# A transformer trunk on one core: residual and transposes between stages in steps of four tiles, norm-weight products in SBUF, turned tiles in PSUM banks 4 to 7

## The reference

```python
def rms_norm(x, g, eps=RMS_EPS):
    xf = x.astype(jnp.float32)
    y = xf * lax.rsqrt(jnp.mean(xf * xf, axis=-1, keepdims=True) + eps)
    return (y * g.astype(jnp.float32)).astype(x.dtype)
...
def conv_ffn(x, w_in, w_dw, w_out):
    u = causal_dwconv(x @ w_in, w_dw)
    g, up = jnp.split(u, 2, axis=-1)
    return (jax.nn.silu(g) * up) @ w_out

def per_layer_embed(h, p_i, pre_g, w_gate, b_gate, w_proj, post_g):
    gate = jax.nn.sigmoid(rms_norm(h, pre_g) @ w_gate + b_gate)
    return rms_norm(gate * (p_i @ w_proj), post_g)
...
    h = x
    for i in range(DEPTH):
        hn = rms_norm(h, pre_mix_g[i])
...
        h = h + rms_norm(y, post_mix_g[i])
        f = conv_ffn(rms_norm(h, pre_ffn_g[i]), ffn_w_in[i], ffn_w_dw[i], ffn_w_out[i])
        h = h + rms_norm(f, post_ffn_g[i])
        h = h + per_layer_embed(h, p[i], ple_pre_g[i], ple_w_gate[i], ple_b_gate[i],
                                ple_w_proj[i], ple_post_g[i])
    return h
```

## Time and profile before

| | us |
|---|---|
| median of 3 runs (2521.71 to 2524.05) | 2522.75 |
| span of the profiled execution, first to last instruction | 2521.0 |
| TensorE busy with products | 2450.2 |
| VectorE busy | 1666.8 |
| ScalarE busy | 1307.0 |

### The profile page before, as it was taken

The page is one execution under the profiler, slowest core; times in us unless marked ns, Lnnn a source line. Parts: engine busy times, 40 slices in busy tenths (PEclk is TensorE's granted clock), DMA queues, the critical chain, the costliest instruction groups (busy, mean ns, idle before and its releaser), DMA issues.

```text
span 2521.0 us, 40724 instructions
## 1 busy us (share of the span) xinstructions
PE 2450.2 (97%) x12610; PEld 2087.9 (83%) x12610; DVE 1666.8 (66%) x2183; ACT 1307.0 (52%) x1882; POOL 27.6 (1%) x49
## 2 busy tenths in 40 slices
PE   7999899999999999999999999999999999999997
PEld 6888787888888888887788887888888888788876
DVE  6889766777777754446665577567777777544465
ACT  6555545555555543436454455465656666433363
POOL 1000000000000000000000000000000000000000
PEclk9999999999999999999999999999999999999999
DMA  6444264666655665555555543646666666655554
GB/s 214 134 128 136 71 195 147 195 191 188 187 185 185 199 201 186 192 189 193 179 180 183 186 151 131 203 150 189 197 191 187 189 185 185 211 189 187 188 195 139
DMA packets 365325, 448.28 MB, mean 178 GB/s; under 512 B 27084, under 2 KB 273726, under 8 KB 364076
## 3 DMA queue, kind: packets, MB, share of 16 engines
q1 hardware_dynamic: 363452, 436.75, 54.5%
q0 software_dynamic: 1776, 10.41, 1.3%
HBM read 444.95 MB, written 2.10 MB: 177 GB/s over the span
## 4 chain that ended last, share of the span: by engine, by line
PE 88%; issue 5%; DVE 3%; ACT 2%; DMA 1%; DVEq 0%; SPq 0%; POOL 0%; ACTq 0%; POOLq 0%
PE ps L1274 34%; PE ps L1276 17%; PE ps L1309 11%; PE ps L1311 11%; PE ps L1310 11%; PE ps L1347 2%; PE ps L1254 1%; DVE v_conv L936 1%; DVE w_lo L809 1%; PE ps L1413 0%; PE ps L1427 0%; DVE h L861 0%; ACT w_hi L504 0%; DMA gain<-in_post_ffn_g 0%; ACT v_conv L610 0%
## 5 line engine op out<-in xcount | busy, mean ns | idle before, releaser
L809 DVE TENSOR_TENSOR w_lo<-raw,w_hi 128x1024 fp32r<-128x1024 f32 x824 | 1002.5, 1224 | 677.7 <-ACT w_hi L504 652.2
L1274 PE MATMUL ps<-x,w_hi 128*128 128x512 f32 x3840 | 1346.5, 395 | 7.9 <-DVE w_lo L809 4.7
L504 ACT CAST w_hi<-raw 128x1024 fp32r<-128x1024 f32 x824 | 859.4, 1049 | 852.3 <-PE ps L1276 425.0
L1276 PE MATMUL ps<-x,w_lo 128*128 128x256 f32 x3840 | 1076.6, 280 | 0.0
L1274 PEld LDWEIGHTS ps<-x,w_hi 128*128 128x128 f32 x3840 | 720.7, 188 | 172.0 <-DVE w_lo L809 5.7
L1276 PEld LDWEIGHTS ps<-x,w_lo 128*128 128x128 f32 x3840 | 727.2, 189 | 0.6
L1309 PE MATMUL ps<-w_hi,mid 128*128 128x512 f32 x704 | 278.1, 395 | 3.0 <-DVE w_lo L809 3.0
L1311 PE MATMUL ps<-w_hi,mid 128*128 128x512 f32 x704 | 277.9, 395 | 0.0
L1310 PE MATMUL ps<-w_lo,mid 128*128 128x512 f32 x704 | 277.9, 395 | 0.0
L1309 PE MATMUL ps<-w_hi,x 128*128 128x512 f32 x640 | 254.9, 398 | 7.1 <-DVE x L981 3.6
L1311 PE MATMUL ps<-w_hi,x 128*128 128x512 f32 x640 | 250.8, 392 | 0.0
(11 more groups left out here) (144 smaller groups left out, 1211.9 us busy)
## 6 DMA issues: line engine op xcount, KB each, us to landing
raw<-in_ffn_w_in SPq DMA_DIRECT2D x704, 256.0 KB, 3.2
raw<-in_ffn_w_out SPq DMA_DIRECT2D x352, 256.0 KB, 3.0
raw<-in_conv_w_pw SPq DMA_DIRECT2D x192, 256.0 KB, 3.2
raw<-in_attn_w_qkv SPq DMA_DIRECT2D x192, 256.0 KB, 2.9
raw<-in_ple_w_gate SPq DMA_DIRECT2D x128, 256.0 KB, 3.4
raw<-in_attn_w_o SPq DMA_DIRECT2D x64, 256.0 KB, 3.3
raw<-in_ple_w_proj SPq DMA_DIRECT2D x16, 256.0 KB, 3.6
h<-in_x SPq DMA_DIRECT2D x4, 512.0 KB, 5.8
```

Source lines behind the costliest of these rows:

```text
L504: nc.scalar.copy(w_hi[:, u % RING], raw[:, u % RING]).then_inc(hi_split, 1)
L809: nc.vector.tensor_tensor(w_lo[:, u % RING], raw[:, u % RING], w_hi[:, u % RING].bitcast(F32), ALU.subtract).then_inc(split_done, 1)
L1274: mm(ps[:, 4 * s + f], w_hi[:, u % RING, q, columns], x[:, kt].rearrange("p a t -> p (a t)"), start=kt == 0, stop=False)
L1276: ins = mm(ps[:, 4 * s + f, 0:T], w_lo[:, u % RING, q, columns], x[:, kt, 0], start=False, stop=kt == KT - 1)
```

## The change

- `y` is the SBUF tensor `z` under another name. `times_gain` reads the product from PSUM and writes it to `y`; `residual` reads `y`. In down the products with the norm weight of chunks 0 to 2 are no longer made behind each chunk but in one group of six in the last chunk, since `y` lies over the first tiles of `mid`, whose last use is in unit 3 of the last chunk.
- The statistic: sum over all but the last chunk, scaled, ahead; when the last sum of squares is there, one instruction adds it.
- Turned tiles lie in banks 4 to 7 in all five transitions (`turned_at`); chunks of four tiles share these banks, so a chunk is turned when the x of the one before is ready. Chunk 0 is turned before the next stage, chunk j + 1 behind unit j (`turn_rest`). `turned` counts each tile.
- The next stage's unit j starts when 2j + 2 tiles of `x` are ready. `early` stays for glu alone.
- `new_h` of both engines works in steps of a chunk, with one weight unit behind each.
- In up, p is turned behind unit 5, in bank 4, and the statistic is spread behind unit 6; in qk behind unit 5; into bank 5.

```diff
-    z = tenant(arena, "z", [P, HALVES, D])
+    z = y = tenant(arena, "z", [P, HALVES, D])
...
+        def turned_at(left, kt):
+
+            return kt if left in ("mix0", "attn") else KT // 2 + 2 * (kt % 4) + kt // 4 % 2
...
             def x_high(left, scale, kts=range(KT)):
 
                 for kt in kts:
-                    if kt % 4 == 0:
-                        act.wait_ge(turned, PIECES * (LEFT[left] - (LEFT[left] > LEFT["ln"])) + kt // 2 + 2)
-                    nc.scalar.activation(x[:, kt, 0], tiles[:, kt], ACT.Copy, scale=scale(kt)).then_inc(x_hi, 1)
+                    act.wait_ge(turned, KT * (LEFT[left] - (LEFT[left] > LEFT["ln"])) + (kt // 4 * 4 + 4 if left in ("mix0", "attn") else kt + 1))
+                    nc.scalar.activation(x[:, kt, 0], tiles[:, turned_at(left, kt)], ACT.Copy, scale=scale(kt)).then_inc(x_hi, 1)
...
-                x_high(left, scale, range(KT // 2))
-                h_squares(left, add, range(PIECES // 2))
-                x_high(left, scale, range(KT // 2, KT))
-                split(None, 0, first + RING, 2)
-                h_squares(left, add, range(PIECES // 2, PIECES))
-                split(None, 0, first + RING + 2, 2)
+                x_high(left, scale, range(0, 4))
+                h_squares(left, add, range(0, 2))
+                x_high(left, scale, range(4, 8))
+                split(None, 0, first + RING, 1)
+                h_squares(left, add, range(2, 3))
+                x_high(left, scale, range(8, 12))
+                split(None, 0, first + RING + 1, 1)
+                h_squares(left, add, range(3, 4))
+                x_high(left, scale, range(12, KT))
+                split(None, 0, first + RING + 2, 1)
+                h_squares(left, add, range(4, PIECES))
+                split(None, 0, first + RING + 3, 1)
...
             def x_low(left, scale, kts=range(KT)):
 
                 for kt in kts:
-                    if kt % 2 == 0:
+                    if left not in ("mix0", "attn"):
+                        dve.wait_ge(x_hi, KT * LEFT[left] + kt + 1)
+                    elif kt % 2 == 0:
                         dve.wait_ge(x_hi, KT * LEFT[left] + kt + 2)
-                    nc.vector.scalar_tensor_tensor(x[:, kt, 1], tiles[:, kt], scale(kt), x[:, kt, 0].bitcast(F32),
...
             def times_gain(k, c, piece_of, last=False):
 
 
                 for half in range(HALVES):
+                    if last and half == 0:
+
+                        dve.wait_ge(stats_done, k + 1)
+                        step.mark(nc.vector.tensor_reduce(ssum[:], stat[:, :, 0:NC - 1], AX_X, ALU.add))
+                        dve.wait_ge(dve_step, step.value())
+                        step.mark(nc.vector.tensor_scalar(ssum[:], ssum[:], 1.0 / D, RMS_EPS, ALU.mult, ALU.add))
                     dve.wait_ge(stats_done, k + (half + 2))
                     if last and half == HALVES - 1:
-                        inverse_root(stat, D)
-                    part = piece_of(half)
-                    step.mark(nc.vector.tensor_tensor(part, part, gain[:, bass.ds(c * UNIT_N, UNIT_N)], ALU.mult))
-
-            def residual(source, pieces):
+                        stats[0] += 1
+                        dve.wait_ge(dve_step, step.value())
+                        nc.vector.scalar_tensor_tensor(meansq[:], stat[:, :, NC - 1], 1.0 / D, ssum[:],
+                                                       ALU.mult, ALU.add).then_inc(var_ready, 1)
+                    step.mark(nc.vector.tensor_tensor(y_rows(c, half), piece_of(half), gain[:, bass.ds(c * UNIT_N, UNIT_N)], ALU.mult))
+
+            def residual(pieces):
 
                 for n in pieces:
-                    c, half, columns = piece(n)
-                    nc.vector.scalar_tensor_tensor(h[:, half, columns], source(c, half), rstd[:, half:half + 1],
+                    _, half, columns = piece(n)
+                    nc.vector.scalar_tensor_tensor(h[:, half, columns], y[:, half, columns], rstd[:, half:half + 1],
                                                    h[:, half, columns], ALU.mult, ALU.add).then_inc(h_updated, 1)
 
-            def new_h(source, left, scale, first):
+            def new_h(left, scale, first):
 
 
                 dve.wait_ge(dve_step, step.value())
                 dve.wait_ge(rstd_ready, stats[0])
-                residual(source, range(PIECES // 2))
-                x_low(left, scale, range(KT // 2))
+                residual(range(0, 2))
+                x_low(left, scale, range(0, 1))
+                residual(range(2, 3))
+                x_low(left, scale, range(1, 3))
+                residual(range(3, 4))
+                x_low(left, scale, range(3, 4))
                 split(None, 0, first + RING - 1, 1)
-                residual(source, range(PIECES // 2, PIECES))
-                x_low(left, scale, range(KT // 2, KT))
-                split(None, 0, first + RING, 2)
+                residual(range(4, 6))
+                x_low(left, scale, range(4, 8))
+                split(None, 0, first + RING, 1)
+                residual(range(6, PIECES))
+                x_low(left, scale, range(8, 12))
+                split(None, 0, first + RING + 1, 1)
+                x_low(left, scale, range(12, KT))
+                split(None, 0, first + RING + 2, 1)
                 dve.wait_ge(hstats_done, PIECES * (HNORM[left] + 1) + 1)
                 inverse_root(hstat, D)
-                split(None, 0, first + RING + 2, 2)
+                split(None, 0, first + RING + 3, 1)
...
-                    split(i, per, first + 2 * RING, FUPC - RING - 1)
-                    times_gain(c * HALVES + PIECES * ADD[f"ffn{layer}"], c, lambda half: ps[:, c * HALVES + half], last)
-                    if not last:
-                        split(i, per, first + FUPC + RING - 1, 1 + RING)
+                    if last:
+                        split(i, per, first + 2 * RING, 2 * UNIT_KT)
+
+                        dve.wait_ge(units_used, used(first + 2 * UNIT_KT))
+                        for earlier in range(NC - 1):
+                            times_gain(earlier * HALVES + PIECES * ADD[f"ffn{layer}"], earlier,
+                                       lambda half: ps[:, earlier * HALVES + half])
+                        split(i, per, first + 2 * RING + 2 * UNIT_KT, FUPC - RING - 1 - 2 * UNIT_KT)
+                        times_gain(c * HALVES + PIECES * ADD[f"ffn{layer}"], c, lambda half: ps[:, c * HALVES + half], True)
+                    else:
+                        split(i, per, first + 2 * RING, FUPC)
...
-                        ins = nc.tensor.transpose(tiles[:, kt, P * half:P * (half + 1)], h[:, half, P * kt:P * (kt + 1)], ident[:])
-                    ins.then_inc(turned, HALVES)
+                        ins = nc.tensor.transpose(tiles[:, turned_at("", kt), P * half:P * (half + 1)], h[:, half, P * kt:P * (kt + 1)], ident[:])
+                        if half == HALVES - 1:
+                            ins.then_inc(turned, 1)
+
+            def turn_rest(add, left, j):
+
+                if j < NC - 1:
+                    pe.wait_ge(x_ready, KT * LEFT[left] + 4 * (j + 1))
+                    turn_h(add, range(j + 1, j + 2))
...
-                if i is None and n == 0:
+                if i is None and n == 0 and left == "mix0":
...
-                        pe.wait_ge(x_ready, KT * LEFT[left] + max(2 * j + 2, KT // 2))
+                        pe.wait_ge(x_ready, KT * LEFT[left] + max(2 * j + 2, KT // 2 if early else 0))
...
-                turn_h(f"mix{layer}", range(NC // 2))
+                turn_h(f"mix{layer}", range(1))
 
                 def embedding_rows(j):
 
-                    if j == 1:
-                        turn_h(f"mix{layer}", range(NC // 2, NC))
-                    if j == 4:
+                    turn_rest(f"mix{layer}", f"ffn{layer}", j)
+                    if j == 5:
+                        pe.wait_ge(x_ready, KT * (LEFT[f"ffn{layer}"] + 1))
                         pe.wait_ge(p_landed, 16 * (layer + 1))
                         for k in range(PLE // P):
                             for half in range(HALVES):
-                                ins = nc.tensor.transpose(tiles[:, 14 + k, P * half:P * (half + 1)],
+                                ins = nc.tensor.transpose(tiles[:, 8 + k, P * half:P * (half + 1)],
                                                           p_rows[:, half, P * k:P * (k + 1)], ident[:])
                         ins.then_inc(p_turned, 1)
-                    if j == 5:
-                        spread_statistic(6, (2, 4)[layer])
+                    if j == 6:
+                        spread_statistic(5, (2, 4)[layer])
...
-                turn_h(f"ffn{layer}", range(NC // 2))
+                turn_h(f"ffn{layer}", range(1))
                 token_chunk(None, place[f"gate{layer}"], lambda half: ps[:, half], f"ple{layer}",
-                            lambda j: turn_h(f"ffn{layer}", range(NC // 2, NC)) if j == 1 else None)
```

(1 more changed line is left out.)

32 lines of the change are left out of this document (15 added, 17 removed).

## The result

The changed kernel takes 2546.51 us, the median of six runs (2525.67 to 2550.01), against 2523.23 us for the kernel before beside it. The ratio on record, which weighs all the runs, is 1.0075 (95% interval 1.0055 to 1.0096); the medians alone differ by 0.92%. The prediction was 2526.6 us with a range up to 2531. Two of the six runs are near it, at 2525.67 and 2532.75; the other four lie at 2546 to 2550. The kernel before spans 2.3 us in its six, and 12.5 us (2514 to 2526.5) over all later runs on several chips. So the first thing to explain is a spread of 24 us in a program whose instructions are the same each time.

A forecast was written before the change was run, and what follows sets the result against it. TensorE, busy 97% of the span, was taken as the bound, so only its waits could be won. Terms gave -0.2 us, plus 4.0 for the clock: +3.8 on a 2521.0 us span, time 2526.6 us, range 2520 to 2531.

The forecast's parts named there:

- statistic 0.20 earlier, six times; first product sooner: Five transitions and program's end: meansq 0.20 us earlier; first product 1.4 us earlier in four transitions, 1.05 in one: -6.85 us.
- eight transposes behind the first product, five times: Each transition: eight transposes move from TensorE's waiting time to between products, 0.84 us each time, +4.2 us.
- wait ahead of the last turn, five times: Ahead of turning chunk 3, TensorE waits for x, 0.45 us in each transition: +2.25 us.
- unit 8 of up later, twice: In up0 and up1 w_lo of unit 8 comes slightly late, 0.1 us each: +0.2 us.
- clock: no early rise at up1 and gate1: After eight transposes the first products at up1 and gate1 run at 1.2 GHz for 3.4 us each: +3.1 us.
- clock in the other three: First three transitions: products begin earlier, partly at the low clock, 0.3 us each: +0.9 us.
- the two early rises: Before, the clock reached 2.4 GHz ahead of the first product at wo to up1 and down1 to gate1; expected lost.
- rival A: Clock costs less: full clock still comes early in the last two transitions: +0.7 us, 2523.4 us; chance 0.20.
- the spread of rstd: In up0 and up1 it moves one unit later, leaving less cover before unit 8: 0.1 us each, 0.2 us.
- B: Slower: clock rises one step later behind first products, 1.5 us each; 2528.1 us for one, 2531.2 for three; chance 0.30.
- C: Faster: clock no longer falls or recovers by the first product, 2517.3 us; or chain waits cost nothing, 2521.1; chance 0.10.
- The edits at nothing: Norm-weight products to SBUF, six in one burst in down, and later loads were claimed to be covered, costing nothing.

The follow-up runs named there:

- e2_y_and_down: Kernel before with y in SBUF, two-step statistic and six early gain products in down's last chunk; turning, banks, spread as before: 2519.7 us, ratio 0.9985.
- e16_y_and_down_again: The kernel of e2_y_and_down unchanged, run again: 2518.73 us, ratio 0.9983 to the kernel before.
- e9_late_cast: Kernel before with four unread ScalarE copies between keeping rstd and the cast of unit 8 in up0 and up1; TensorE's list unchanged: 2541.27 us, ratio 1.0075.
- e6_one_unit_later: Kernel before with only the embedding's rows and the rstd spread in up0 and up1 moved behind units 5 and 6: 2540.1 us, ratio 1.0069.
- e5_one_unit_earlier: Changed kernel with the embedding's rows and the rstd spread in up put back behind units 4 and 5: 2528.78 us, ratio 1.0034.
- e12_two_more: e2_y_and_down plus two unread products behind unit 4 of the second chunk of up0 and up1, that chunk written out: 2539.81 us, ratio 1.0065.
- e1_after_again: Changed kernel with no edit, run again for a profile of another execution: 2542.81 us, ratio 1.0071.

## Why the prediction was wrong, step by step

**The sum was near for what it priced, in part by luck.** In the short execution, against the trace of before:

| step | predicted us | measured us |
|---|---|---|
| statistic 0.20 earlier, six times; first product sooner | -6.85 | -6.6 |
| eight transposes behind the first product, five times | +4.2 | +3.95 |
| wait ahead of the last turn, five times | +2.25 | +1.8 |
| unit 8 of up later, twice | +0.2 | +1.5 |
| clock: no early rise at up1 and gate1 | +3.1 | +4.6 |
| clock in the other three | +0.9 | -0.6 |
| sum; spans | +3.8 | +4.7; +2.8 |

The statistic: from the last square on ScalarE to the first residual it is 1.80 us in down0 to gate0 (1142.59 to 1144.39) where it was 2.00. At the end of the program the 0.20 us did not come: from the last sum of squares on ScalarE to the residual it is 1.81 us against 1.83, since a norm-weight product holds VectorE. From first residual to first product the five transitions take 4.56, 4.51, 4.55, 4.20 and 4.25 us against 5.69, 4.97, 5.69, 5.68 and 5.63: 5.6 us, and 1.0 for the statistic. Per place the forecast was off both ways: the second gained 0.46 us where 0.85 was expected, the last two 1.5 and 1.4 where it was 1.2. The transposes: 5 x 0.79. The waits: the row of 1.8 us above. The clock: the stretches at 0.50 behind the first products of up1 and gate1 are 5.7 and 4.4 us, at 0.456 us each; that is over the forecast's own bound of 4.0. In the other three they went from 3.9, 4.4 and 3.3 us to about 3.3, 3.4 and 3.5. What is left between sum and spans are differences between the two executions outside these steps: down1 is 2.1 us shorter in the trace of the changed kernel (249.1 us against 251.2, from its first product to the first transpose behind it).

That the two early rises would not come behind eight transposes was the forecast's side of its choice against rival A, and it held: in the seven traces with eight transposes there, no first product has the full clock. But they are no fixed part of the kernel before either. In the eleven traces with 16 transposes ahead, the first product has the full clock nine times at wo to up1 and five times at down1 to gate1, and of the two traces of one kernel, e2_y_and_down and e16_y_and_down_again, only the second has it at gate1. So the price of 3.1 us was read from a favourable trace. By the Trainium skill (TensorE: Matmul & The Clock Gate, Part 4) transposes do not engage the full clock. The traces disagree, since it rose with nothing but 16 transposes behind the wait, and with eight it did not. The forecast for such an execution, 2526.6 us, stands beside runs at 2525.67 and 2527.36.

**The step that failed is the spread of rstd.** I wrote "I put 0.1 us each, between 0 and 0.3: 0.2 us". Two things were wrong in it. The smaller: it was worked out from up0, where it held (0.05 us), and carried over to up1, where ScalarE's table load of 1.28 us lies in the same chain, and unit 8 came 1.46 us late. The larger: I priced the interruption by its own length. Behind it TensorE runs 1344 pairs of products without a break, and their pace depends on how TensorE entered them. e9_late_cast has that wait alone and loses 18 us, e6_one_unit_later has that part of the change alone and loses 18 us; the changed kernel loses 20 to 23.

**The second step that failed** is the silent one: moved transposes, products and waits were counted by their durations, as though what runs behind them kept its pace. The late spread is not the only part that does it. With the spread put back (e5_one_unit_earlier) the up loops are still slow in some executions, behind turns and waits that the change has put elsewhere. In e5_one_unit_earlier's profiled execution the spread of up0 came behind a pair with 0.233 us and that of up1 behind one with 0.236, as the table above has it. Why the changed kernel varies from run to run is not shown. In both its traces the product at unit 8 of up0 is 0.05 us late, within 0.002 us of each other, and one came out fast and the other slow. That such a wait makes the spread is a guess: e6_one_unit_later ends in the same wait in up1 and spans 3.4 us in its five runs, and e12_two_more, which has none, spans 11.6.

**The rivals.** None of them explains the 20 us. B had the sign, and its mechanism is there, but small: in the short execution the clock rose later in one of the five (5.7 us at 0.50 in up1), in e1_after_again the stretches are 5.7, 5.2, 4.4, 5.6 and 4.8 us. One row of that trace, first transition:

```profile
401.00:406.70 5.70, 5.70 (x19) 4.93 (x20) 3.75 (x6) 0.73 (x2) 0.00 (x0) 0.50 0.31 91
```

At 0.456 us for each this is 2.5 us between the two executions. C's "waits in the chain cost nothing" was nearly right for the chain, and no help.

**The edits at nothing** held: TensorE's waits for w_lo ahead of products of down, gate and wo add up to 2.1 us in the trace of the changed kernel and 3.6 in that of before, so the burst in down made none in that execution; and e2_y_and_down and e16_y_and_down_again, which contain them all, gain 2.8 and 3.6 us at the median, more than the 1.2 of the statistic. Where the rest comes from was not followed.

## What to carry to other kernels

Where one engine runs a long loop back to back, look at the pace in the loop, not only at the waits: count the instructions in equal windows of two traces. A small instruction or a wait well under a microsecond ahead of such a loop can set its pace for hundreds of microseconds, so an edit there is worth what a measured run says, in several executions, and not its own length. Moves in the bound engine's list should be kept apart from edits on the other engines: here the second kind alone beats the kernel before.
